# Running sums from halves in the weights' format, and a new order of weight halves in a two-layer transformer kernel

## The reference, cut to what matters

```python
z = einsum('bhqd,bhkd->bhqk', q, k) * scale
causal = s_pos < t_pos
log_keep = where(causal, log_sigmoid(-z), 0.0)
later = cumsum(log_keep, axis=3, reverse=True) - log_keep
a = where(causal, exp(log_sigmoid(z) + later), 0.0)
out = einsum('bhqk,bhkd->bhqd', a, v)
```

## Time and profile before

| | before |
|---|---|
| median of 3 runs | 923.9 us |
| the profiled execution: its own time / its span | 924.6 / 923.0 us |
| TensorE busy | 906.6 us (98%), 7210 matmul records |
| VectorE busy | 674.5 us (73%) |
| ScalarE busy | 475.4 us (52%) |
| GpSimd busy | 57.1 us (6%) |
| mean granted TensorE clock | 0.998 |
| read from HBM | 152.52 MB, 166 GB/s over the span |

### The profile page before, as it was taken

The page is one execution under the profiler, slowest core; times in us unless marked ns, Lnnn a source line. Parts: engine busy times, 40 slices in busy tenths (PEclk is TensorE's granted clock), DMA queues, the critical chain, the costliest instruction groups (busy, mean ns, idle before and its releaser), DMA issues.

```text
span 923.0 us, 17806 instructions
## 1 busy us (share of the span) xinstructions
PE 906.6 (98%) x7210; PEld 870.7 (94%) x7210; DVE 674.5 (73%) x1194; ACT 475.4 (52%) x836; POOL 57.1 (6%) x124
## 2 busy tenths in 40 slices
PE   8999999999999999999999999999999999999997
PEld 7899989999999999997999988999999999999996
DVE  7764576778877877888799886786657666666686
ACT  5355354555655455466366644564336544444466
POOL 5022000120000000000000000000102000000001
PEclk9999999999999999999999999999999999999999
DMA  8543444545456556555644464565555566666651
GB/s 313 182 151 103 136 137 120 184 138 180 145 180 193 181 175 197 181 176 156 205 138 138 131 174 130 159 187 181 183 160 182 185 197 187 185 184 183 184 159 46
DMA packets 42688, 154.71 MB, mean 168 GB/s; under 512 B 4720, under 2 KB 5232, under 8 KB 42480
## 3 DMA queue, kind: packets, MB, share of 16 engines
q1 hardware_dynamic: 42608, 153.59, 53.7%
HBM read 152.52 MB, written 1.05 MB: 166 GB/s over the span
## 4 chain that ended last, share of the span: by engine, by line
PE 86%; DVE 8%; ACT 3%; issue 2%; DMA 1%; SPq 0%; POOL 0%; DVEq 0%; ACTq 0%
PE bank L266 86%; DVE wl L1306 3%; ACT wh L863 1%; DMA raw<-in_wts 1%; DVE work L1695 0%; DVE work L1676 0%; ACT work L1116 0%; DVE wh L1302 0%; DVE tmpb L1887 0%; DVE xc L1889 0%; DVE tmpb L1612 0%; DVE work L1693 0%; DVE tmpb L1608 0%; ACT qk L1269 0%; DVE qk L1714 0%
## 5 line engine op out<-in xcount | busy, mean ns | idle before, releaser
L1306 DVE TENSOR_TENSOR wl<-raw,wh 128x1024 fp32r<-128x1024 f32 x284 | 351.7, 1247 | 109.2 <-ACT wh L863 107.4
L863 ACT ACTIVATE wh<-raw 128x1024 fp32r<-128x1024 f32 x249 | 259.9, 1052 | 163.5 <-PE bank L266 151.4
L266 PE MATMUL bank<-a2h,wh 128*128 128x256 f32 x896 | 254.2, 284 | 0.6 <-DVE wl L1306 0.6
L266 PE MATMUL bank<-a2h,wl 128*128 128x256 f32 x896 | 250.5, 280 | 0.0
L266 PE MATMUL bank<-a2l,wh 128*128 128x256 f32 x896 | 248.7, 280 | 0.0
L266 PE MATMUL bank<-a1h,wh 128*128 128x258 f32 (+1 forms) x800 | 226.8, 285 | 2.2 <-DVE wl L1306 1.2
L266 PE MATMUL bank<-a1h,wl 128*128 128x258 f32 (+1 forms) x800 | 224.0, 282 | 0.0
L266 PE MATMUL bank<-a1l,wh 128*128 128x258 f32 (+1 forms) x800 | 220.5, 282 | 0.0
L266 PEld LDWEIGHTS bank<-a2h,wh 128*128 128x128 f32 x896 | 168.9, 188 | 3.9 <-issue 2.7
L266 PEld LDWEIGHTS bank<-a2h,wl 128*128 128x128 f32 x896 | 168.8, 188 | 0.0
L266 PEld LDWEIGHTS bank<-a2l,wh 128*128 128x128 f32 x896 | 167.7, 188 | 0.3
(11 more groups left out here) (239 smaller groups left out, 990.8 us busy)
## 6 DMA issues: line engine op xcount, KB each, us to landing
raw<-in_wts SPq DMA_DIRECT2D x284, 512.0 KB, 3.7
csb<-in_cst SPq DMA_DIRECT2D x1, 1428.0 KB, 11.3
out<-va SPq DMA_DIRECT2D x2, 512.0 KB, 3.0
xc<-in_xT SPq DMA_DIRECT2D x1, 544.0 KB, 7.2
raw<-in_wts SPq DMA_DIRECT2D x2, 256.0 KB, 3.4
xc<-in_xT SPq DMA_DIRECT2D x1, 276.0 KB, 3.1
xc<-in_xT SPq DMA_DIRECT2D x1, 272.0 KB, 4.4
va<-in_pT SPq DMA_DIRECT2D x1, 256.0 KB, 3.9
```

Of the source, the lines that this page charges most:

```text
L266: return e.matmul(o, lhsT, rhs, start=start, stop=stop, skip_group_check=True)
L863: e.activation(wh[:, i % NHL, :], raw[:, i % NRAW, :], ACT.Copy).then_inc(s_hi, 1)
L1306: e.tensor_tensor(lo, src, hi.bitcast(F32), ALU.subtract).then_inc(s_lo, 1)
```

## The change

Running sums: `negu` is copied once into an fp32r tile `negr`. For each stick-breaking head ScalarE rounds the masked softplus to a high half (`sb_hi`, j=4) and VectorE makes the low half (`sb_lo`, j=3); TensorE multiplies `negr` with both in place of the float32 product. The sums move to j=6, the values to 8, the heads out to 9. The two smaller products stay float32.

Orders: VectorE makes both halves of block 1, and SyncE waits for the first tokens before it issues the third token transfer; `lo_to`/`hi_to` calls move at the FFN's start, at the second layer's value blocks and at its output projection; the root per token is made on VectorE (a masked reduction with the identity) and no longer by 1x1 matmuls; steps of differential heads 6 and 7 move; every second retention sum goes to bank 3.

```diff
 def by_vector(i):
-    return i % 8 == 4 and i < B_GP
+    return i == 1 or i % 8 == 4 and i < B_GP
...
+        SB_AH = lambda h: a1h[:, 0:4, :].rearrange("p a b -> p (a b)")[:, 418 * (h % 2):418 * (h % 2) + 418]
+        SB_AL = lambda h: a1l[:, 0:4, :].rearrange("p a b -> p (a b)")[:, 418 * (h % 2):418 * (h % 2) + 418]
+        RET_SUM = lambda h: bank[B_S2[0] if h % 2 else B_T2][:, 0:S]
...
             def sb_cumsum(h):
-                e.wait_ge(s_mk, 3 * h + 3)
-                mm(z[:, 0:418], negu, a, False, False)
+                e.wait_ge(s_negr, 1)
+                e.wait_ge(s_alo, h + 1)
+                mm(z[:, 0:418], negr[:, :], SB_AH(h), False, False)
+                mm(z[:, 0:418], negr[:, :], SB_AL(h), False, False)
                 mm(z[:, 114:258], negone, a[:, 258:402], False, False)
... TensorE, value_root: the n == 6 branch goes
-                    for b in range(2):
-                        t = mm(bank[2][:, S + b:S + b + 1], rb[0:1, 0, b * 128:b * 128 + 128], ones[0:1, 0:1], False, True)
...
             def ret_sum(h):
                 e.wait_ge(s_rqa, h + 1)
-                if h:
-                    e.wait_ge(s_rln, h)
-                mm(bank[B_T2][:, 0:S], ones, qk[:, 8 + 2 * h, 0:S], True, True).then_inc(s_rss, 1)
+                if h % 2:
+                    e.wait_ge(s_rp, 3)
+                if h >= 2:
+                    e.wait_ge(s_rln, h - 1)
+                mm(RET_SUM(h), ones, qk[:, 8 + 2 * h, 0:S], True, True).then_inc(s_rss, 1)
... ScalarE
+            def sb_hi(h):
+                e.wait_ge(s_mk, 3 * h + 3)
+                if h >= 2:
+                    e.wait_ge(s_cum, h - 1)
+                e.activation(SB_AH(h), SB_A(h), ACT.Copy).then_inc(s_ahi, 1)
...
-                    elif k == 4 and n == 1:
-                        hi_to(B_V2 + 4)
+                    elif k in (4, 6) and n == 1:
+                        hi_to(B_V2 + (4 if k == 4 else 5))
...
                         if j:
-                            hi_to(i + 4)
+                            hi_to({(2, 0): B_FF + 10, (3, 0): B_FF + 12}.get((j, half), i + 4))
...
+                        if (j, half) == (1, 0):
+                            hi_to(B_FF + 9)
... after residual_hi(1, ...)
+            hi_to(B_V2 + 6)
...
-                    elif a == 2:
+                    elif a == (0 if h == 6 else 2):
                         diff_square(h)
...
-            for m in range(9):
-                if 3 <= m < 8:
-                    hi_to(B_WOUT2 + m + 4)
...
+            for m in range(8):
                 if m:
+                    hi_to(B_WOUT2 + max(m + 4, 6))
... VectorE
+                if k == 3:
+                    lo_to(2)
                 input_lo(k)
...
+            def sb_lo(h):
+                e.wait_ge(s_ahi, h + 1)
+                if h >= 2:
+                    e.wait_ge(s_cum, h - 1)
+                low(SB_AL(h), SB_A(h), SB_AH(h)).then_inc(s_alo, 1)
... loop over m of layer 1's output projection
+                if m == 7:
+                    lo_to(B_FF + 3)
                 e.wait_ge(s_sqa, 4 + m + 1)
...
-            lo_to(B_FF + 3)
             add_normed(0, ...
... up_out(n)
-                lo_to(B_FF + 6 if n == 1 else i + 4)
+                lo_to({1: B_FF + 6, 3: B_FF + 8, 4: B_FF + 9, 5: B_FF + 10, 6: B_FF + 11, 7: B_FF + 12}.get(n, i + 4))
...
-            e.wait_ge(s_rt, 1)
-            e.tensor_copy(r_tok, bank[2][:, S:S + 2]).then_inc(s_rtc, 1)
+            for b in range(2):
+                e.tensor_tensor_reduce(tmpb[:, b, 0:128], rb[:, 0, b * 128:b * 128 + 128], ident, 1.0, 0.0, ALU.mult, ALU.add,
+                                       r_tok[:, b:b + 1]).then_inc(s_rtc, 1)
...
-                    elif a == 1:
+                    elif a == (0 if h == 6 else 1):
                         diff_clamp(h)
... proj2 of VectorE
-                lo_to(i + 4)
+                if t != 20:
+                    lo_to(i + 4)
                 pump2(p)
+                if t == 20:
+                    pump2(p + 1)
... eviction of tile t
-                pump2(p + 1)
+                if t == 20:
+                    lo_to(i + 4)
+                else:
+                    pump2(p + 1)
... second output projection
+            lo_to(B_WOUT2 + 4)
+            for m in range(3):
+                mix_out(m)
             lo_to(B_WOUT2 + 5)
+            for m in range(8):
+                if m >= 3:
+                    mix_out(m)
                 if m:
+                    lo_to(B_WOUT2 + max(m + 4, 6))
+                weighed_lo(N_UP2, m, ...
... SyncE
             load(1)
+            e.wait_ge(s_x[0], 16)
             tokens(2, KT + 4 * L, KT + 8 * L)
```

More of the change, by code:

```diff
@@ L74, in by_vector @@
 def by_vector(i):
-    return i % 8 == 4 and i < B_GP
+    return i == 1 or i % 8 == 4 and i < B_GP
 def hid_count(i):
-    return (min(i, B_GP - 1) + 4) // 8
+    return (min(i, B_GP - 1) + 4) // 8 + (1 if i >= 1 else 0)
 N_GATES = 16
@@ L155, in program @@
         selr = sb("selr", [104, 8], F32R)
+        negr = sb("negr", [P, 128], F32R)
+        SB_AH = lambda h: a1h[:, 0:4, :].rearrange("p a b -> p (a b)")[:, 418 * (h % 2):418 * (h % 2) + 418]
+        SB_AL = lambda h: a1l[:, 0:4, :].rearrange("p a b -> p (a b)")[:, 418 * (h % 2):418 * (h % 2) + 418]
         lamb = gr[:, 0, :].rearrange("p (a b) -> p a b", a=4)
@@ L896, in scalar_engine @@
             e.activation(selr[:, :], csb[0:104, C_SEL:C_SEL + 8], ACT.Copy).then_inc(s_selr, 1)
+            e.activation(negr[:, :], negu, ACT.Copy).then_inc(s_negr, 1)
             def forget():
@@ L965, in pump1 @@
                         sb_log(h)
-                    elif j == 5:
+                    elif j == 4:
+                        sb_hi(h)
+                    elif j == 6:
                         sb_exp(h)
-                    elif j == 8 and h % 2:
+                    elif j == 9 and h % 2:
                         heads_hi(h // 2, 4 + h // 2)
@@ L1154, in ret_root @@
                     e.wait_ge(s_rn, 2 * h - 2)
-                e.activation(r, bank[B_T2][:, 0:S], ACT.Ln, bias=eps, scale=1.0 / 256).then_inc(s_rln, 1)
+                e.activation(r, RET_SUM(h), ACT.Ln, bias=eps, scale=1.0 / 256).then_inc(s_rln, 1)
                 e.wait_ge(s_rln, h + 1)
@@ L1231, in scalar_engine @@
             hi_to(B_WOUT2 + 5)
-            for m in range(9):
-                if 3 <= m < 8:
-                    hi_to(B_WOUT2 + m + 4)
+            for m in range(8):
                 if m:
[L1236 to L1240, removed]
+                    hi_to(B_WOUT2 + max(m + 4, 6))
+                e.wait_ge(s_x2, m + 1)
+                weighed_hi(m, a1h[:, m, 0:S], xk(m), COL_GMLP)
+                if m >= 5:
+                    e.wait_ge(s_sqp, Q_UP2 + m - 4)
+                e.activation(qk[:, 2 if m == 0 else 3 + m % 4, 0:S], xk(m), ACT.Square).then_inc(s_sqa, 1)
             hi_to(B_FF2 + 4)
@@ L1300, in lo_to @@
                         e.wait_ge(s_raw[i % NRAW], 16 * (i // NRAW + 1))
-                        e.wait_ge(s_blk, i - NHL + 1)
+                        if i >= NHL:
+                            e.wait_ge(s_blk, i - NHL + 1)
                         e.tensor_copy(hi, src).then_inc(s_hid, 1)
@@ L1473, in pump1 @@
                         sb_softplus(h)
-                    elif j == 8 and h % 2:
+                    elif j == 3:
+                        sb_lo(h)
+                    elif j == 9 and h % 2:
                         heads_lo(h // 2, 4 + h // 2)
@@ L1830, in vector_engine, with mix_out @@
             mix_lo(N_MIX2, 7, a2h, a2l)
-            lo_to(B_WOUT2 + 5)
-            for m in range(9):
-                if m < 8:
-                    if m >= 3:
-                        lo_to(B_WOUT2 + m + 4)
-                    e.wait_ge(s_blk, B_WOUT2 + m + 1)
-                    e.tensor_tensor(xk(m), xk(m), bank[W_OUT_BANK(m)][:, 0:S], ALU.add).then_inc(s_x2, 1)
+            def mix_out(m):
+                e.wait_ge(s_blk, B_WOUT2 + m + 1)
+                e.tensor_tensor(xk(m), xk(m), bank[W_OUT_BANK(m)][:, 0:S], ALU.add).then_inc(s_x2, 1)
+            lo_to(B_WOUT2 + 4)
+            for m in range(3):
+                mix_out(m)
+            lo_to(B_WOUT2 + 5)
+            for m in range(8):
+                if m >= 3:
+                    mix_out(m)
                 if m:
-                    weighed_lo(N_UP2, m - 1, a1l[:, m - 1, 0:S], a1h[:, m - 1, 0:S], xk(m - 1), COL_GMLP)
+                    lo_to(B_WOUT2 + max(m + 4, 6))
+                weighed_lo(N_UP2, m, a1l[:, m, 0:S], a1h[:, m, 0:S], xk(m), COL_GMLP)
             lo_to(B_FF2 + 5)
```

16 lines of the change are left out of this document (8 added, 8 removed).

## The result

The changed kernel takes 915.75 us in the median of four runs (914.87 to 917.04) against 923.9 us (923.79 to 924.06) for the kernel before: a ratio of 0.9913, with a 95% interval of 0.9896 to 0.9930. Forecast were 914.9 us and a range of 912.4 to 918.6. The profiled execution took 915.08 us with a span of 913.9 us, 9.2 us less than the span before (923.04 less 913.85 in the traces).

A forecast was written before the change was run, and what follows sets the result against it. The prediction took TensorE, busy 98% of the span, and its stops to bound the kernel. Its terms summed to -9.0 us, taking the median from 923.9 to 914.9 us, range 912.4 to 918.6.

The forecast's parts named there:

- head 7: Seventh differential head: the stop before its turn moves down to block 157 and grows; +0.3 us (-1.0 to +0.8).
- running sums: Stick-breaking heads: four fp32r matmuls replace the large float32 products, 0.65 us saved per pair, four pairs; -2.6 us.
- block 1: First weight blocks: VectorE makes the high half faster than ScalarE plus hand-over; -0.4 us (-0.2 to -0.9).
- FFN start: Block 65: low half made one eviction earlier, so TensorE's stop there goes; -1.4 us (-0.6 to -1.6).
- value blocks: Layer 2: the wait at block 129 goes (1.5 us), masked reductions replace 1x1 matmuls (0.6); -2.1 us together.
- second projection: Second output projection: block 210's high half comes one step earlier, ending TensorE's stop; -0.8 us (-0.5 to -1.1).
- End of the first projection: First output projection: block 60's cast moves before the last copy, TensorE starts earlier; -0.3 us (-0.1 to -0.4).
- Retention sums: Retention heads: a second bank lets every second sum start 0.82 us earlier, twice; -1.7 us (-1.4 to -1.8).
- The value blocks from 157 wait for just this eviction: Step in the head 7 term: tile 22's eviction on VectorE, delayed, sets block 157's start, forecast at 534.5.
- Rival 1: Head 7's stop goes without a successor because eviction 22 is in time; 913.6 us, chance 0.20.
- Rival 2: FFN start and value blocks keep most stops, block 1 and 210 bring half; 918.0 us, chance 0.22.
- Rivals 3 and 4: Running sums: fp32r products at float32 distance, 923.3 us (chance 0.03); sums late behind slow masks, 925.7 us (0.02).

The follow-up runs named there:

- head7_mended: Changed kernel with tile 22 turned too: head 5's scale (VectorE) and root (ScalarE) before block 158's low and high halves; median 913.12 us.
- before_again: The kernel before, unaltered, profiled once more; 925.48 us.
- after: First profile of the changed kernel, nothing else altered; the profiled execution took 915.08 us.
- after_third: The changed kernel, unaltered, profiled a third time; 915.52 us.
- head7_steps_old: Changed kernel with only head 6's clamp and square put back at their old steps, VectorE's new order at tile 20 kept; median 915.16 us.
- before: First profile of the kernel before, without the change; the profiled execution took 924.6 us.

## Why the prediction came out as it did

The sum said -9.0 us; the spans gave -9.2, the medians -8.15. The closeness in the spans is luck: blocks 68 to 122 took 155.40 us in the profile before and 154.32 in the profile after, and both kernels have either. Without these 1.08 us the change brings 8.1 us, as the medians do. Behind that, head 7 came out 1.1 us worse than its term, and the running sums and block 1 0.3 and 0.2 worse; the FFN start, the value blocks and the second projection came out 0.2 to 0.3 us better each. Term by term, from the table:

- **Running sums**, -2.6 forecast, -2.32 measured. The mechanism held: four fp32r matmuls for the large float32 ones, no wait for a half. A pair takes 60.52 - 58.90 = 1.62 us, and the product itself costs 0.187 us, as priced. The cost before was read from the last pair, 2.25 us; the three others took 2.35, so the sums' own matmuls save 2.8 us in all. But 0.5 us of it go again, and the prediction had no term for this: before, the next pair's float32 score products followed these three sums directly; with the sums one step later, products on the weights stand between them. Where such products give way to float32 ones or take over again, TensorE needs 0.20 to 0.23 us to the next start where 0.12 is usual. Between blocks 13 and 25 there are 18 such places where there were 12. The scores behind the first pair's sums before, and a place after (60.52 to 60.73):

```profile
58.73 0.71 PE L266 MATMUL bank<-qk,gr 64*128 64x258 f32 x4
...
60.73 0.29 PE L272 MATMUL bank<-xnl,wh 128*128 128x272 f32 x1
```

- **Block 1**, -0.4 forecast, -0.18 in the profile after, about -0.5 in the means of fourteen. The chain from the high half on is shorter by 0.30 to 0.37 us, as priced; the rest is when the block lands. Whether SyncE's new wait matters wasn't tried by itself.
- **End of the first projection and FFN start**, -0.3 and -1.4 forecast; -1.95 in all for blocks 50 to 68, of which 0.34 at the projection.
- **Value blocks**, -1.5 and -0.6 forecast; -1.50 and -0.82, 0.73 of that by the 1x1 matmuls.
- **Retention sums**, -1.7 forecast, -1.71 measured. **Second projection**, -0.8 forecast, -1.10 measured: the sum counted only the stop at block 210, while the blocks right behind it, up to the start of 213, gained 0.3 too.
- **Head 7**, +0.3 forecast, +1.39 measured. This is the term that was mis-sized. The chain was followed to the right instant: shifted by the 7.81 us that had been gained by then, its low half of 158 was due at 525.09 and its eviction at 526.22, and the trace has 525.07 and 526.21. The step that failed is the next one, "The value blocks from 157 wait for just this eviction". Behind the eviction VectorE still owes head 5's scale (526.55 to 526.97), and head 7's value products wait for that and take 0.65 us before block 157. TensorE was thus held earlier and longer, one matmul group ahead of the place I watched; the passage at block 157 itself is unbroken, which the prediction had listed as a sign of wrong. The forecast of block 157, 534.5 - 7.81 = 526.7, is 1.07 us short of 527.76, nearly the whole error of the term (1.09).

Rival 1 (no successor of the stop) is what `head7_mended` makes of the kernel, not what the change did. Rival 2 (orders that run dry) did not come: blocks 65, 129 and 210 start at once. Rivals 3 and 4 are excluded by the 0.187 us a product and by low halves that end 1.7 us or more before the sums in all four pairs; the first pair's masks took 1.31 us (1.44 before).

The terms for the FFN start, for block 129 and for the retention sums are read from their stages, in which the stops are gone; these orders weren't undone one by one.

What stays open: why the same matmuls take 154.32 us in one execution and 155.40 in another, at a granted clock of 1.00, and whether that has to do with the clock's fall behind head 7's stop.

## What to carry to other kernels

When a step is moved to end a stop, follow each displaced queue on until the *first* matmul that waits for anything in it, not until the next weight block: the order at tile 20 took away 1.07 us and cost 2.3 two tiles later, and one more turned pair there made it a gain. Price a change stage by stage from block to block, and compare several profiles of both kernels before a drift over a long stage is put to the change. A stop costs its length and, here in three of six executions, up to another 1.5 us of half clock behind it.

## What the hardware showed that was not expected

- **The clock falls behind a stop in some executions only.** Of the six profiles with TensorE's bracket of 2.0 to 2.2 us at head 7, three have the clock at 1.2 GHz for some 3 us afterwards (4.42, 4.43 and 4.01 us for block 157) and three do not. It also fell behind the wait for block 1 in `before_again` (2.08 us), and in all fourteen profiles at the very end, around TensorE's last matmuls (in `after` these start at 908.31 and the clock falls at 908.9), where it costs next to nothing. Behind the other stops, which last up to 1.71 us, it did not fall.
- **More than one pace at one clock.** Blocks 68 to 122 took 154.32 us in nine profiles and 155.40 us in five, in kernels with the same code there, and the retention blocks 170 to 190 took 57.16 us in `after`, 57.76 in `after_third` and 58.37 in `head7_steps_old`. `before` and `before_again`, the stretch from 260 to 400 us, differ mainly in the count of matmuls in it:

```profile
260.00:400.00 140.00, 140.00 (x1170) 140.00 (x1169) 111.48 (x187) 72.69 (x109) 0.00 (x0) 1.00 0.59 185
```

```profile
260.00:400.00 140.00, 140.00 (x1178) 140.00 (x1177) 112.41 (x188) 72.10 (x108) 0.00 (x0) 1.00 0.59 185
```
